# Attention mixer: GpSimd takes the further convolution taps of one of four channel chunks

## The reference

```
q  = rms_norm(rms_norm(p[:384]) @ w_uq, per head), k likewise from p[384:640] and a shared rotary part kpe
attn = softmax(q k^T * scale, with a chunk-causal mask) @ v          # 8 heads, 256 tokens
u = a * sigmoid(g)                                                   # 512 channels
y[t, c] = conv_b[c] + sum over k = 0..30 of u[t - 30 + k, c] * conv_w[k, c]
conv = silu(layer_norm(y))
x = x + concat([attn, conv]) @ w_out
```

## Time and profile before

| | |
|---|---|
| median of 3 runs | 2495.82 us (2495.55 to 2497.08) |
| profiled execution | 2496.97 us, of which 2494.9 us are the span |
| TensorE busy | 2398.4 us, 96% |
| VectorE busy | 1901.2 us, 76% |
| ScalarE busy | 1442.9 us, 58% |
| GpSimd busy | 27.2 us, 1% |
| chain that ended last | TensorE 89%, VectorE 8%; the taps (L2056) 2% |

### The profile page before, as it was taken

One profiled execution on the slowest core, in us unless ns is written; L12 is line 12 of the kernel. 1 busy time (PEld: TensorE's weight loads), 2 busy tenths in 40 slices (PEclk: granted clock), 3 DMA queues, 4 the chain that ended last, 5 costly groups with the idle time before them and its releaser, 6 DMA issues.

```text
span 2494.9 us, 33483 instructions
## 1 busy us (share of the span) xinstructions
PE 2398.4 (96%) x12192; PEld 2020.1 (81%) x12192; DVE 1901.2 (76%) x1951; ACT 1442.9 (58%) x1489; POOL 27.2 (1%) x49
## 2 busy tenths in 40 slices
PE   5999999999999999999999989998999999998998
PEld 5888888788888888888888778885888788867886
DVE  5676677888888888888888866679666766696765
ACT  3544445677777677767777754445544544555543
POOL 3000000000000000000000000000000000000000
PEclk9999999899999999999999989998999999997999
DMA  5555554699989999999899945542355455432552
GB/s 198 188 186 185 185 171 167 248 372 343 371 341 372 342 371 342 372 340 371 343 371 342 372 148 193 187 140 94 129 191 186 162 190 191 163 125 85 180 190 84
DMA packets 83869, 594.37 MB, mean 238 GB/s; under 512 B 9920, under 2 KB 10242, under 8 KB 12626
## 3 DMA queue, kind: packets, MB, share of 16 engines
q1 hardware_dynamic: 81216, 587.76, 64.8%
q0 software_dynamic: 2000, 4.50, 0.6%
q10 hardware_dynamic: 582, 1.16, 0.1%
HBM read 592.33 MB, written 1.05 MB: 238 GB/s over the span
## 4 chain that ended last, share of the span: by engine, by line
PE 89%; DVE 8%; ACT 1%; DMA 1%; issue 1%; ACTq 0%; DVEq 0%
PE banks L1036 17%; PE banks L1087 9%; PE banks L1089 9%; PE banks L1093 9%; PE banks L1038 8%; PE banks L1112 8%; PE banks L1114 8%; PE banks L1113 8%; DVE acc L2056 2%; PE banks L1065 2%; DVE lo L1626 2%; PE banks L1209 1%; PE banks L1128 1%; DMA stage_rows<-in_sgu_b 1%; PE banks L1335 1%
## 5 line engine op out<-in xcount | busy, mean ns | idle before, releaser
L1626 DVE TENSOR_TENSOR lo<-raw,hi 128x2048 fp32r<-128x2048 f32 x550 | 1258.4, 2290 | 229.8 <-ACT hi L557 224.6
L557 ACT CAST hi<-raw 128x2048 fp32r<-128x2048 f32 x550 | 1051.6, 1912 | 251.9 <-PE banks L1093 119.0
L1036 PE MATMUL banks<-xhl,hi 128*128 128x512 f32 x1776 | 632.7, 400 | 0.7 <-DVE lo L1626 0.4
L1038 PE MATMUL banks<-xhl,lo 128*128 128x256 f32 x1776 | 499.8, 281 | 0.0
L1036 PEld LDWEIGHTS banks<-xhl,hi 128*128 128x128 f32 x1776 | 335.0, 189 | 84.9 <-DVE lo L1626 2.0
L1112 PE MATMUL banks<-hi,xhl 128*128 128x512 f32 x896 | 354.5, 396 | 0.8 <-issue 0.8
L1114 PE MATMUL banks<-hi,xhl 128*128 128x512 f32 x896 | 350.4, 391 | 0.0
L1113 PE MATMUL banks<-lo,xhl 128*128 128x512 f32 x896 | 349.6, 390 | 0.0
L1087 PE MATMUL banks<-hi,hh 128*128 128x512 f32 x872 | 343.0, 393 | 1.8 <-DVE hl L1638 1.8
L1089 PE MATMUL banks<-lo,hh 128*128 128x512 f32 x872 | 340.7, 391 | 0.0
L1038 PEld LDWEIGHTS banks<-xhl,lo 128*128 128x128 f32 x1776 | 336.8, 190 | 1.9
(11 more groups left out here) (373 smaller groups left out, 2448.3 us busy)
## 6 DMA issues: line engine op xcount, KB each, us to landing
raw<-in_moe_w_gate SPq DMA_DIRECT2D x112, 1024.0 KB, 4.9
raw<-in_moe_w_up SPq DMA_DIRECT2D x112, 1024.0 KB, 4.9
raw<-in_moe_w_down SPq DMA_DIRECT2D x112, 1024.0 KB, 4.9
raw<-in_ffn_w_gate SPq DMA_DIRECT2D x58, 1024.0 KB, 4.9
raw<-in_ffn_w_up SPq DMA_DIRECT2D x58, 1024.0 KB, 4.9
raw<-in_ffn_w_down SPq DMA_DIRECT2D x58, 1024.0 KB, 4.9
raw<-in_mix_pieces SPq DMA_DIRECT2D x46, 1024.0 KB, 4.9
raw<-in_mix_pieces SPq DMA_DIRECT2D x2, 768.0 KB, 4.1
```

Source lines behind the costliest of these rows:

```text
L557: nc.scalar.copy(hi[:, hslot(S, c), 0:n], raw[:, c % RING, 0:n]).then_inc(S.hi_done, 1)
L1036: pe.matmul(bank[b + s][:, :], hi[:, hr, a:a + P], xhl[:, k, :], start=(k == 0), stop=False, skip_group_check=True)
L1038: mm = pe.matmul(bank[b + s][:, 0:T], lo[:, r, a:a + P], xhl[:, k, 0:T], start=False, stop=(k == KD - 1), skip_group_check=True)
L1626: v.tensor_tensor(lo[:, c % RING, 0:n], raw[:, c % RING, 0:n], hi[:, hslot(S, c), 0:n].bitcast(F32), ALU.subtract).then_inc(S.lo_done, 1)
```

## The change

GpSimd computes taps 1 to 30 of chunk 0 in both attention mixers. Each tap is a product into one half of `tap` and an addition to `acc`, and after each operation but the last GpSimd waits for it. `tap` lies in `xn`. It starts when ScalarE has done the first tap of chunk 0 (`gate_act`). After tap 24 it waits for the end of the q projection and issues the mask DMA, then does the last six taps and signals `pooled_out`. TensorE waits for that before the transposes of `acc`, and VectorE before it writes `xn`. VectorE's list starts with chunk 0 marked as done, and the numbers of taps after the heads' maxima are dealt out anew. Calls for chunk 0 alone stay in the code and issue nothing.

```diff
+MASK_TAP = 24
+        tap = xn[:, 0, 0:2 * T].rearrange("p (n t) -> p n t", n=2)
@@ pe_mix2
             pe.wait_ge(ev("conv31_out"), l + 1)
+            pe.wait_ge(ev("pooled_out"), l + 1)
@@ GpSimd
+            def mix2_work(st, l):
+                pool.wait_ge(x_done, 4 * st["M"])
+                pool.wait_ge(ev("gate_act"), 8 * l + 2)
+                for k in range(1, CK):
+                    link(g.tensor_scalar(tap[:, k % 2, :], upad[:, 0, k:k + T], col(("cw2", l), 4 * k), None, ALU.mult))
+                    ins = g.tensor_tensor(acc[:, 0, :], acc[:, 0, :], tap[:, k % 2, :], ALU.add)
+                    if k < CK - 1:
+                        link(ins)
+                    if k == MASK_TAP:
+                        pool.wait_ge(main.multiplied, st["B"] + 9)
+                        pool.dma_start(qkT[QK:KEYS, :, :], hide).then_inc(ev("mask_in"), 16)
+                ins.then_inc(ev("pooled_out"), 1)
-            for g in range(2):
-                pool.wait_ge(ev("xg_done"), TT * (g + 1))
-                load_gain(2 + g)
-                B = next(st["B"] for st in stages if st["kind"] == "mix2" and st["layer"] == g)
-                pool.wait_ge(main.multiplied, B + 9)
-                pool.dma_start(qkT[QK:KEYS, :, :], hide).then_inc(ev("mask_in"), 16)
+            for l in range(2):
+                pool.wait_ge(ev("xg_done"), TT * (l + 1))
+                load_gain(2 + l)
+                st = next(st for st in stages if st["kind"] == "mix2" and st["layer"] == l)
+                mix2_work(st, l)
@@ mix2 on VectorE
-                done, tap_at, ready = [1] * 4, [0] * 4, [0, 1, 2]
+                done, tap_at, ready = [CK, 1, 1, 1], [0] * 4, [1, 2]
-                    conv((3, 3, 2, 8, 2, 8, 8, 8)[h], ready)
+                    conv((3, 3, 4, 6, 2, 6, 6, 6)[h], ready)
                 dve.wait_ge(ev("att_out"), 8 * (l + 1))
+                dve.wait_ge(ev("pooled_out"), l + 1)
```

## The result

The changed kernel takes 2510.75 us (median of 4 runs, 2507.91 to 2512.26). The kernel before, run beside it, takes 2495.72 us (2495.55 to 2497.08). The ratio is 1.0059 (1.0047 to 1.0072), so it is 15.0 us slower. The forecast was 2519 us: the direction and the range hold, and the loss was put 8.3 us too high (+23.3 from the median, +15.0 measured). The mean granted clock is 0.976 in both profiles.

What follows compares the result with a forecast made beforehand. Nearly all is TensorE work; in the mixers VectorE is as busy as anything, delaying q projection and heads. Per layer +12.6 + 2.3 - 3.1 = +11.8, twice +23.6 on 2496.97: 2520.6, less 1.15: 2519 us; range 2487 to 2532.

Steps and rivals of the forecast that it cites:

- place A: Start of the q projection (L1387): TensorE waits for `kpe`, computed by VectorE behind its taps; idle 1.75 us in layer 0.
- place B: The heads: VectorE does fixed taps between heads' maxima; TensorE idles 1.30 (twice) and 2.69 us for the exponentials behind them.
- Exclusion, VectorE held as well as GpSimd: In the mixers, GpSimd's SBUF reads and VectorE's two-input SBUF operations exclude each other; VectorE loses 0.74 us per GpSimd tap.
- Rival 1: Beside VectorE's taps: VectorE is never held and GpSimd fills gaps; 7.9 us faster, 2488 us; chance 0.27.
- rival 2: Before the heads: a small loss, 0.2 to 0.45 us per tap, pays back the heads' gain; 2492 to 2500; chance 0.12.
- rival 3: Beside VectorE's taps: VectorE always wins, GpSimd starves, mask and scores come late; +22 per layer, 2540; chance 0.08.
- GpSimd's own durations: GpSimd's taps: multiply 0.39 us, add 0.59, 0.24 between operations; 1.46 undisturbed, 1.86 among VectorE's taps.
- `kpe` 12.6 us late: Before the q projection: VectorE's work stretches by 1.66 beside GpSimd's taps, so `kpe` comes 12.6 us later in either layer.
- The uncontended gain of 1.7 us in layer 0: Before the q projection, without contention: VectorE's taps start earlier, so `kpe` gains 1.7 us in layer 0, 0 in layer 1.
- The clock, +2.3 us: q projection: TensorE's granted clock falls during the long wait; some 2.3 us until it is back, bounds 0 and 8.
- Heads, -3.1 us: Heads 3, 5 and 6 lose two VectorE taps each, 3.1 us less per layer; heads 0 to 2 gain nothing.
- The mask: Mask DMA issued by GpSimd still goes out when the q projection ends, tap 24 being past; no L1424 wait for it.

Runs made afterwards that it cites:

- e1: Changed kernel with GpSimd's 60 operations per layer taken out, chunk 0's further taps left out altogether; 2487.28 us, ratio 0.997 to the kernel before.
- e3: Changed kernel with each GpSimd tap replaced by three memsets of 128x512, which read nothing from SBUF; 2486.61 us, ratio 0.9965 to the kernel before.
- e11: Kernel before, nothing on GpSimd, five VectorE taps moved from the heads into its wait for the first scores; 2488.61 us, ratio 0.9973.
- e4: Changed kernel with each GpSimd add replaced by a second one-input multiply; 2502.93 us, ratio 1.0029 to the kernel before.
- e2: Kernel before's VectorE list with all 120 taps, plus GpSimd's 60 operations per layer on spare data; 2530.65 us, ratio 1.0141.
- e5: Changed kernel with each GpSimd multiply replaced by a second two-input add; 2513.11 us, ratio 1.0068 to the kernel before.

## Why the prediction was right, and where its size was off

**What bounds the kernel, place A and place B: right.** The loss stands at the q projection waiting for `kpe`, in both layers, and the gain in the heads. (In layer 1, e1 starts the q projection only 0.2 us earlier than the kernel before, close to the 0 that was forecast.)

**Exclusion, VectorE held as well as GpSimd: right, and its price near by luck.** It was argued from GpSimd's side alone; one of its rows is weak, because the iota of 13.18 to 13.42 lies mostly between the two subtractions (10.77 to 13.06 and 13.32 to 15.61). e3 gives what it was to show. VectorE and GpSimd thus meet not only at semaphores but also at their reading of SBUF. In the 24 taps that don't depend on one another the stretch is 14.95 / 9.59 = 1.56 (forecast 1.66). With a GpSimd tap every 1.88 us it is 5.36 / 7.95 = 0.67 us lost for each, where the prediction took 0.74 from between 0 and 0.98. But the 0.74 was the full length of both operations, put at 0.98, less 0.24 of pauses. With the lengths that were measured (0.97 + 0.73) the same rule gives 1.46 us, more than twice the loss: lengths that were too short made up for a hold that was taken as too complete. Rival 1 (never held, 2488) is excluded by the 0.67, and rival 2 (0.2 to 0.45 us) as well; rival 3 (GpSimd starves) too, since GpSimd kept 1.88 us.

**GpSimd's own durations: right in sum, wrong in the parts.** The forecast had 0.39 for the multiply, 0.59 for the add, 0.24 between operations, 1.46 alone and 1.86 with VectorE's taps. Measured are 0.93 to 0.97, 0.73, 0.08 to 0.10 and 1.84 to 1.88. The select and the memset were no measure for a multiply by a scalar from memory. Too short an operation, too long a gap, and a wait for VectorE that hardly exists made up for one another. That the sum of 1.86 came out is luck as well.

**`kpe` 12.6 us late: the step that was mis-sized.** It is 10.0 us late. Against e1, where GpSimd does nothing, `kpe` comes 10.75 us later, and the 2.65 us that the `lo` piece waits there for its cast are used up too: VectorE lost 13.4 us to 23 GpSimd taps, 0.58 each. The forecast had 12.6 + 1.7 + 2.4 = 16.7 to 24, 0.70 each. Place by place, changed kernel against e1: the nine taps of one chunk 1.48, the 24 taps 5.36, the `lo` piece 0.53, the 20 taps 4.00, L2097 0.71, and 1.39 behind them. The largest error is in the first: the factor 1.66 was laid on taps that wait for each other. There each engine waits for the other (GpSimd's adds take 0.85 us, its taps 2.0), and VectorE loses (6.13 - 4.65) / (6.13 / 2.0) = 0.48 us for each of them and not 0.74. That is 1.6 of the 3.3 us; another 1.0 is the 24 taps' factor. The prediction also had GpSimd at tap 24, and VectorE free, 2.2 us before `kpe`. In fact GpSimd's tap 24 began at 1706.03 and `kpe` at 1705.94, so nothing before the q projection was free of GpSimd.

**The uncontended gain of 1.7 us in layer 0: half wrong.** The `lo` piece does start 1.65 us earlier in e1 than before, as worked out, but `kpe` only 0.7. The 20 taps behind it take 8.62 us instead of 8.00: chunk 1 has had nine taps more, is used up first, and the last taps are all of one chunk, which wait for one another. The prediction had priced this for the first nine taps and not for the last.

**The clock, +2.3 us: right.** +1.8 and +2.4 us in the q projection.

**Heads, -3.1 us: right, slightly small.** 3.6 us, and e11 shows that they don't come from GpSimd. The 3.1 us lie where they were forecast, behind the maxima of heads 3, 5 and 6. The other 0.5 us are heads 0 to 2, which were put at nothing: 0.4 and 1.3 us won in heads 0 and 1, 1.2 lost in head 2.

**The mask: right.** GpSimd stood at tap 24 at 1707.76, waited 9.07 us, and no score waited for the DMA. e4 shows how little was left: there GpSimd's 24 taps took 54.0 us instead of 47.8, and the scores wait 3.4 us.

**The sum.** Measured by stretches +8.2 and +8.8 (forecast +11.8 each): `kpe` 2 x 2.6 us less, the heads 2 x 0.5 and the clock 2 x 0.2, in all 6.6 of the 8.3 us between forecast and result. The rest is the 2 us between the stretches' +17.0 and the medians' +15.0. The two profiled executions are 13.4 us apart, of which 3.1 us less lie ahead of layer 0's mixer and 0.5 us less between the mixers, where both kernels do the same. The one of the kernel before is 1.3 us above its median and starts that mixer later than every other trace of this study (by 0.1 to 3.1 us). So I take the 2 us for the spread of executions; that wasn't tested.

## What to carry to other kernels

Before work is moved from VectorE to GpSimd, compare what the moved instruction costs VectorE in either place. Here a tap costs VectorE 0.40 us when it does it itself and 0.48 to 0.67 us when GpSimd does it beside two-input SBUF operations, so the move loses on the busy engine even though GpSimd was busy 1% of the time. Look next at which of the engine's own instructions could go into its waits: two lines (e11) gave all that GpSimd was called in for.

## What the runs showed of the hardware

- A GpSimd multiply of 128x256 by a scalar per partition is recorded with 0.92 to 0.98 us but costs VectorE's two-input SBUF operations only 0.20 us; an add of 0.67 costs them 0.35 us, one of 0.73 us 0.48. A memset costs nothing (9.60 against 9.59 us for 24 taps).
- A VectorE tap that starts during a GpSimd add ends 0.28 us after the add's end, in e2, e5 and the changed kernel alike; beside a multiply it ends 0.17 us before the multiply's end.
- Not only operations with two inputs are held. In the changed kernel a VectorE multiply-and-add of 128x2 with one SBUF input (L2137) took 0.69 us instead of 0.16 and ended 0.03 us after a GpSimd add.
- It is one-sided with short instructions that don't depend on one another: VectorE's taps stretch by 56%, GpSimd's by 2% (1.84 to 1.88 us). With dependent taps it is 32% against 9% (2.0 us). With a VectorE instruction of 2.29 us it turns: GpSimd's operation lasts 2.5 to 3.1 us, the VectorE one at most 0.53 longer.
- VectorE operations with one input in PSUM and the other in SBUF kept 0.42 us beside GpSimd.
